# Rotary swap of queries and keys done by 32-row transfers inside SBUF, and the hyena projection's column pairs taken in another order with the transposition moved into its stage

## The reference, cut to what matters

```
q, k, v, g, hy_u, gate_ret, gate_hy = split(h @ w_in + b_in, ...)
# retention: 4 heads of 128 for q and for k; each head is rotated in two halves of 64
def rope_1d(x, ang):                       # x: 64 wide, ang: 32 wide
    x1, x2 = x[..., :32], x[..., 32:]
    return concat([x1 * cos - x2 * sin, x1 * sin + x2 * cos])
q_h = rope_grid(q);  k_h = rope_grid(k) * 128 ** -0.5
...
# hyena: u = hy_u is 1536 wide, three parts of 512
x0, x1, v = split(short_conv(u, conv_w, conv_b), 3)     # 3 taps along the tokens, plus a bias
z = x1 * v
y = long_conv(z) + z * skip
out = x0 * y
```

## Time and profile before

| | us |
|---|---|
| median of 3 runs (lowest, highest) | 4257.39 (4257.15, 4257.42) |
| the profiled execution's own time | 4258.63 |
| its span, first to last instruction | 4256.8 |
| PE busy in the span | 3793.8 (89%) |
| DVE busy | 1520.0 (36%) |
| ACT busy | 1015.0 (24%) |
| mean granted clock of PE (1 is full) | 0.959 |

### The profile page before, as it was taken

One profiled execution on the slowest core, in us unless ns is written; L12 is line 12 of the kernel. 1 busy time (PEld: TensorE's weight loads), 2 busy tenths in 40 slices (PEclk: granted clock), 3 DMA queues, 4 the chain that ended last, 5 costly groups with the idle time before them and its releaser, 6 DMA issues. The chain is left out here.

```text
span 4256.8 us, 96995 instructions
## 1 busy us (share of the span) xinstructions
PE 3793.8 (89%) x42177; PEld 2439.0 (57%) x42177; DVE 1520.0 (36%) x2645; ACT 1015.0 (24%) x2384; POOL 604.8 (14%) x748
## 2 busy tenths in 40 slices
PE   7998899989999889999978998978888799996995
PEld 2443447874444478888854444447777644445774
DVE  5456225552112410000042666545555512222003
ACT  3200100040011122222243442034454211112333
POOL 1120000001100000000010001235555211000112
PEclk9999999999999889999989999989999999997998
DMA  8352311203112389999961001100000111206998
GB/s 293 131 163 79 121 59 60 79 12 70 42 34 93 121 310 393 394 390 395 398 219 25 9 3 45 40 6 5 4 4 4 64 48 52 98 37 226 384 388 317
DMA packets 242335, 597.53 MB, mean 140 GB/s; under 512 B 37097, under 2 KB 149640, under 8 KB 222123
## 3 DMA queue, kind: packets, MB, share of 16 engines
q1 hardware_dynamic: 200867, 471.27, 30.4%
q0 software_dynamic: 19120, 73.68, 5.0%
q10 hardware_dynamic: 22104, 49.00, 3.4%
HBM read 522.85 MB, written 71.05 MB: 140 GB/s over the span
## 5 line engine op out<-in xcount | busy, mean ns | idle before, releaser
L1790 PE MATMUL experts_bank<-experts_uT,ex_wu 128*64 128x96 f32 x9216 | 389.9, 247 | 25.9 <-PE experts_bank L1776 22.2
L1790 PEld LDWEIGHTS experts_bank<-experts_uT,ex_wu 128*64 128x64 f32 x9216 | 383.6, 137 | 42.7 <-issue 42.7
L1863 DVE TENSOR_TENSOR experts_hT<-experts_si,experts_bank 128x384 f32<-128x384 f32 (+1 forms) x68 | 31.3, 460 | 723.6 <-PE experts_bank L1790 723.6
L1790 PE MATMUL experts_bank<-experts_uT,b2z_hT 128*64 128x96 f32 x4096 | 179.1, 249 | 27.3 <-DMA b2z_hT<-in_w 14.8
L1790 PEld LDWEIGHTS experts_bank<-experts_uT,b2z_hT 128*64 128x64 f32 x4096 | 173.4, 139 | 42.2 <-issue 42.2
L1776 PE MATMUL experts_bank<-mixed_T,experts_hT 128*32 128x256 f32 (+1 forms) x2592 | 193.9, 451 | 0.0
L1776 PEld LDWEIGHTS experts_bank<-mixed_T,experts_hT 128*32 128x32 f32 x2592 | 110.4, 110 | 69.6
L1818 ACT ACTIVATE experts_uT<-experts_bank,all_modrun 128x96 f32<-128x96 f32 x296 | 99.3, 439 | 211.6 <-PE experts_bank L1771 211.6
L2413 POOL TENSOR_TENSOR b2z_hT<-b2z_hT,rwkv_level 128x256 f32<-128x256 f32 x192 | 140.2, 763 | 44.3 <-DVE b2z_hT L2892 33.5
L1399 DVE TENSOR_TENSOR merge_u<-merge_bank,merge_sg 128x512 f32<-128x512 f32 x16 | 11.1, 692 | 340.1 <-PE merge_bank L1332 340.1
L3294 PE MATMUL mh_sc<-mla_KTs,mh_QT 128*128 128x512 f32 x256 | 120.7, 594 | 5.9 <-ACT mla_KTs L3339 5.9
(11 more groups left out here) (618 smaller groups left out, 7264.0 us busy)
## 6 DMA issues: line engine op xcount, KB each, us to landing
ex_wu<-in_expert_w SPq DMA_DIRECT2D x72, 2048.0 KB
mixed_T<-in_expert_w SPq DMA_DIRECT2D x36, 2048.0 KB
b2z_hT<-in_w SPq DMA_DIRECT2D x64, 1024.0 KB
b2z_Z<-in_w SPq DMA_DIRECT2D x32, 1024.0 KB
keep_rows<-mix_hyT ACTq DMA_DIRECT2D x27, 768.0 KB, 8.7
keep_rows<-experts_yo ACTq DMA_DIRECT2D x68, 288.0 KB
mix_hT<-in_ada_w POOLq DMA_DIRECT2D x8, 2048.0 KB, 11.8
vg_w<-in_w_in SPq DMA_DIRECT2D x32, 512.0 KB, 4.5
```

Of the source, the lines that this page charges most:

```text
L1790: last = pe.matmul(bk[2 + j][c:c + 64, h * BT:(h + 1) * BT], wu[:, s, j, k, h * P + c:h * P + c + 64], uT[:, s, k, :], start=(k == 0), sto ...
```

## The change

**Queries and keys.** The matrix `rot`, its load and the 8 rotation products of each step are gone. The sign now sits in the sine table (`k_rope1`). When ACT has moved both halves of tile n to `qk`, it waits until DVE is done with tile n-1 and starts four transfers of 32 rows by 1024 columns (128 KB each) from `qk` to `t[:, 1, :]`, each pair of 32-row groups crossed. DVE makes the cosine product meanwhile, waits for the four transfers (`swapped`), makes the sine product over the whole tile in place, and adds. The loops are written out instead of counted, and the phase uses four banks instead of eight; a tile's weights are asked for when the tile two before it is done.

**Hyena.** The six column pairs are taken in the order 2, 4, 3, 5, 0, 1, so x1 and v come first and x0 last. As soon as a tile of v is made, DVE multiplies the tile of x1 by it. Behind the last pair's products and folds PE transposes the gated tiles in the same block, into the same eight banks. For the last pair ACT makes the first tap of both tiles, the tile that is folded first going first, and DVE the other two; then ACT copies the eight banks to `zn`. `phase_hyena_turn` is gone.

```diff
 def phase_qk(...)
         @b.sync
...
+            for n in range(2, TILES):
+                sp.wait_ge(done, 2 * (n - 1))
+                sp.dma_start(wt[:, n % 2, :, :], w[:, :, n * P:(n + 1) * P]).then_inc(wfull[n % 2], 16)
...
         @b.tensor
         def _(pe):
-            pe.sem_inc(wfree, 2)
-            pe.wait_ge(come, 32)
-            with pe.Fori(0, STEPS) as i:
...
-                for s in range(2):
-                    pe.wait_ge(roped, i * 2 + (s + 1))
-                    pe.wait_ge(evac, i * 4 + (2 * s + 6))
-                    for h in range(2):
-                        last = pe.matmul(bk[4 + 2 * s + h][:, :], rot, one(qk[:, bass.ds(i * 2 + s, 1), h * HALF:(h + 1) * HALF]), start=True, stop=True)
-                    last.then_inc(swapped, 1)
+            for n in range(TILES):
+                pe.wait_ge(wfull[n % 2], 16 * (n // 2) + 16)
+                if n >= 2:
+                    pe.wait_ge(evac, 2 * (n - 1))
+                for h in range(2):
+                    for k in range(KT):
+                        last = pe.matmul(bk[2 * (n % 2) + h][:, :], wt[:, n % 2, k, :], xT[:, k, hs[h]], start=(k == 0), stop=(k == KT - 1))
+                    last.then_inc(done, 1)
 
         @b.scalar
...
+            for n in range(TILES):
+                for h in range(2):
+                    act.wait_ge(done, 2 * n + h + 1)
+                    act.activation(qk[:, n, hs[h]], bk[2 * (n % 2) + h][:, :], ACT.Identity, bias=K.cols[:, bcol + n:bcol + n + 1]).then_inc(evac, 1)
+                act.wait_ge(evac, 2 * n + 2)
+                if n:
+                    act.wait_ge(roped, n)
+                for q in range(4):
+                    here, there = 32 * q, 32 * (q ^ 1)
+                    act.dma_start(t[here:here + 32, 1, :], qk[there:there + 32, n, :]).then_inc(swapped, 16)
 
         @b.vector
...
+            for n in range(TILES):
+                scale = sc[:, n // RH:n // RH + 1]
+                dve.wait_ge(evac, 2 * n + 2)
+                if n:
+                    dve.wait_ge(roped, n)
+                dve.scalar_tensor_tensor(t[:, 0, :], qk[:, n, :], scale, cs[:, 0, :], ALU.mult, ALU.mult).then_inc(turned, 1)
+                dve.wait_ge(swapped, 64 * (n + 1))
+                dve.scalar_tensor_tensor(t[:, 1, :], t[:, 1, :], scale, cs[:, 1, :], ALU.mult, ALU.mult).then_inc(turned, 1)
+                dve.wait_ge(turned, 2 * n + 2)
+                dve.tensor_tensor(qk[:, n, :], t[:, 0, :], t[:, 1, :], ALU.add).then_inc(roped, 1)
 
 def phase_taps(...)
+    ORDER = (2, 4, 3, 5, 0, 1)
...
         def _(pe):
             for p in range(npairs):
                 pairs.products(pe, p)
+            pe.wait_ge(gated, 4)
+            pe.wait_ge(pairs.copied, npairs)
+            pe.wait_ge(pairs.folded, 7 * npairs)
+            for par in range(2):
+                for mt in range(4):
+                    for c in range(4):
+                        src = zc[:, 4 + c, :].rearrange("p (n two) -> p two n", two=2)[:, par, mt * P:(mt + 1) * P]
+                        last = pe.transpose(bk[par * 4 + mt][:, c * P:(c + 1) * P], src, K.ident[:, :])
+                    last.then_inc(tr, 1)
 
         @b.scalar
...
+            for n in (1, 0):
+                t = 2 * ORDER[end] + n
+                act.wait_ge(pairs.folded, 7 * end + (6 if n else 7))
+                act.activation(zc[:, t, :], up[:, n, 0:SEQ], ACT.Identity, scale=tap(0, t), bias=tap(3, t)).then_inc(tapped, 1)
+            for n in range(8):
+                act.wait_ge(tr, n + 1)
+                act.activation(zn[:, n, :], bk[n][:, :], ACT.Copy).then_inc(moved, 1)
             act.wait_ge(asided, 16 * len(aside))
 
         @b.vector
...
+                    if p < end:
+                        then(dve.tensor_scalar(o, up[:, n, 0:SEQ], tap(0, t), tap(3, t), ALU.mult, ALU.add))
+                    else:
+                        dve.wait_ge(tapped, x + 1)
...
+                    if t >= 8:
+                        then(last)
+                        dve.tensor_tensor(zc[:, t - 4, :], zc[:, t - 4, :], o, ALU.mult).then_inc(gated, 1)
 
 def constants():
-    c["k_rope1"] = np.stack([np.cos(ang), np.sin(ang)], 1).astype(f)
+    c["k_rope1"] = np.stack([np.cos(ang), sgn * np.sin(ang)], 1).astype(f)
```

More of the change, by code:

```diff
@@ L498, in _ @@
         @b.scalar
         def _(act):
-            act.sem_inc(evac, 4)
-            with act.Fori(0, STEPS) as i:
-                for s in range(2):
-                    for h in range(2):
-                        hold(act, done, i * 4 + (2 * s + h + 1))
-                        act.activation(one(qk[:, bass.ds(i * 2 + s, 1), h * HALF:(h + 1) * HALF]), bk[2 * s + h][:, :], ACT.Identity,
-                                       bias=K.cols[:, bass.ds(i * 2 + (s + bcol), 1)]).then_inc(evac, 1)
+            for n in range(TILES):
[8 more added lines that the diff above has]
+                    act.dma_start(t[here:here + 32, 1, :], qk[there:there + 32, n, :]).then_inc(swapped, 16)
@@ L508, in _ @@
         @b.vector
         def _(dve):
[L510 to L511 removed]
+            dve.wait_ge(come, 16)
             dve.wait_ge(scale_ok, 2)
[L513 to L527 removed]
+            for n in range(TILES):
[8 more added lines that the diff above has]
+                dve.tensor_tensor(qk[:, n, :], t[:, 0, :], t[:, 1, :], ALU.add).then_inc(roped, 1)
@@ L1943, with __init__ @@
     M1, M2, M4, M6, M7, M5, M3 = range(1, 8)
-    def __init__(self, m, hT, slab, bk):
+    def __init__(self, m, hT, slab, bk, order=range(8)):
+        self.order = order
         self.bk, (self.b11, self.b12), (self.b21, self.b22) = bk, *quarters(hT)
@@ L2047, in phase_taps @@
         bk = m.banks(8)
-        pairs = Pairs(m, xT, slab, bk)
-        zero, chain, asided = m.sems("zero", "chain", "asided")
+        pairs = Pairs(m, xT, slab, bk, ORDER)
+        zero, chain, asided, gated, tr, tapped, moved = m.sems("zero", "chain", "asided", "gated", "tr", "tapped", "moved")
         b = m.block()
         each = -(-len(aside) // npairs)
+        end = npairs - 1
         @b.sync
@@ L3655, in constants @@
     sgn = np.concatenate([-np.ones(32), np.ones(32)] * 2)[:, None]
-    c["k_rope1"] = np.stack([np.cos(ang), np.sin(ang)], 1).astype(f)
-    rot = np.zeros((128, 128))
-    for d in range(128):
-        src = d + 32 if d % 64 < 32 else d - 32
-        rot[src, d] = sgn[d, 0]
-    c["k_rot1"] = rot.astype(f)
+    c["k_rope1"] = np.stack([np.cos(ang), sgn * np.sin(ang)], 1).astype(f)
     return c
```

89 lines of the change are left out of this document (19 added, 70 removed).

## The result

| | us |
|---|---|
| median of 4 runs (lowest, highest) | 4213.61 (4209.61, 4219.78) |
| before, beside it: median of 4 runs (lowest, highest) | 4257.27 (4253.63, 4257.42) |
| ratio (95% interval) | 0.9903 (0.9889, 0.9916) |
| span of the profiled execution | 4218.0 |

The kernel is faster by about 1%, 41.3 us (35.8 to 47.3) by the ratio.

A forecast was written before the change was run, and what follows sets the result against it. Serial work between barriers was taken as the bound, PE setting the pace in queries and keys: 18.2 + 13.3 - 1.1 = 30.4 us off 4258.63, less 1.24 for the median, gives 4227.0; range 4223 to 4231, with slow covered swaps 4222 to 4237.

The forecast's parts named there:

- what their ends move by, the total moves by: Changed phases lie one behind the other between barriers, so the total shifts as their ends do; forecast 30.4 us less.
- the 2 us that the range allowed for the phases behind: Allowance either way in the range, because half-speed stretches in the phases behind may fall otherwise.
- 18.2 forecast: Queries and keys: without rotation products and loop waits, the next phase starts at 638.1 instead of 656.27, minus 18.2 us.
- The rule of the Trainium skill: Queries-and-keys swaps: rows 0 to 31 reach half the ports, two transfers nearly serialize; about 4.8 us, total 0.7 longer.
- the row: Profile row for 512 KB stored from SBUF, 2.6 us, taken as the landing of the last tile's four transfers.
- The cover: Queries and keys: a tile's swap and sum take 6.7 of PE's 13.75 us, so seven of eight tiles cost nothing.
- the clock term: Convolution's start: PE idles nearly 8 us instead of 6.15, so a longer half-clock stretch; plus 1.1 us.
- 13.3 was forecast: Hyena projection's end: ACT's last copy ends at 325.5 instead of 338.78, minus 13.3 us.
- Slow, covered swaps: Queries and keys: landing 8.7, issues 1.33, only the last tile pays; 4235.6 us in total; chance 0.12.
- the bounds: Upper bounds for queries-and-keys swaps: landing 8.7 us, issues 1.33 us each; the saving there falls to 9.6 us.
- Swaps as the bound: Queries and keys: swap loop outlasts PE's tile; 4284 us at X = 20; chance 0.04 slower, 0.04 no difference.
- Hyena saves nothing: Hyena projection's end: copies to `zn` or half-speed transposes eat the gain; at worst 3.5 us; no chance given.

The follow-up runs named there:

- e4: Changed kernel with eight fills of a spent tile on GpSimd at the end of queries and keys; ratio 0.9925, median 4225.1 us.
- e5: The kernel before, unaltered, profiled a second time; 3595.7 us from values and gates to the span's end.
- e16: The changed kernel unaltered, third profile; ratio 0.9911, median 4212.97 us.
- e1: The kernel before with only the hyena part of the change; ratio 0.9962.
- e2: The kernel before with only the queries-and-keys (swap) part of the change; ratio 0.9932.
- e8: The kernel before with its queries-and-keys loop written out on four engines, rotation products kept; ratio 0.9991.
- e15: The kernel before with the queries-and-keys loop written out and PE's rotation products left out, table still loaded; ratio 1.0033.
- e9: The changed kernel without the 32-row transfers, so the rotation is left out; ratio 0.9979.
- e12: The changed kernel with the last tile swapped by halves and the convolution's first table requested early; ratio 0.9893, 4211.0 us.
- e3: The changed kernel unaltered, second profile; ratio 0.9912, median 4219.6 us.
- e6: The changed kernel with each of a tile's four transfers cut into four, 16 requests per tile; ratio 0.9937.

## Why the prediction was wrong, and where it was right

**What failed** is the first step, "what their ends move by, the total moves by", and the 2 us that the range allowed for the phases behind. The ends moved by what was forecast, within 2.2 us, and e4 shows that what lies behind starts as much later as the phase ends later; but it also became shorter, by some 8.6 us (the means 3597.0 and 3588.4). 30.4 + 2.2 + 8.6 = 41.2, and 41.3 was measured. That this closes so well is luck, because the two repeats gave 37.5 and 37.9. 5 of the 8.6 lie in the chunks: 569.0 on average with the old products, 563.9 in thirteen profiles with the new code, and PE's issue time there fell by about 6. The rest is spread; no other phase behind differs by more than 1.2 us in the mean. The waits of PE in the chunks, for e5 and for e16 (waited for: total, times, longest):

```profile
PE rc_banks L2433 <- issue: 47.0, 72, 1.6
PE rc_banks L2433 <- DVE rc_xy L2901: 11.8, 12, 2.7
```

```profile
PE rc_banks L2421 <- issue: 38.4, 61, 1.3
PE rc_banks L2421 <- DVE rc_xy L2889: 11.6, 10, 2.9
```

The longest waits for DVE are the same; what shrinks is PE's wait for its own instructions. Why it shrinks is open. It goes with the products in the old loop (e1, e2, e8, e15), but the same edits shift the 256-record places, and that rival is untested. It isn't the loop's form alone, the transfers or the table. Nor is it the chip: three chips ran both codes (e1 to e4, e5 to e8, e9 to e12), with 47.0 to 50.7 us for the old one and 39.4 to 48.7 for the new, e3 being the one above 44. And even without this, untouched phases drift by 5 to 10 us from profile to profile of one kernel (3584.1 to 3593.8 for the changed one), so 2 us was too little for a range.

**Queries and keys: right, to the tenth by some luck.** 18.2 forecast, 18.3 measured. 110.1 us of projections were forecast as 8 x 13.75 + 0.2 = 110.2; the tail from the first request to the sine product was 1.47 + 0.1 + 2.6 = 4.17, measured 4.19. The parts differ and make up for each other: ACT needs 0.51 to 0.94 us per request, so the fourth starts 1.84 us behind the first and not 1.47, but it lands 2.33 us after its start and not 2.6. The rule of the Trainium skill that stood against this ("SBUF — State Buffer", "Door 1: The DMA port swizzle") gave an estimate of 4.8 us from the first issue; the trace says 4.19, nearer to the row than to the rule. But the estimate adds 2 us of fixed time to a rate that the Trainium skill gives there as measured at 1 MiB, so it can count that time twice, and one chain of 4.19 doesn't decide between row and rule. The cover holds as said, with one tile in which DVE waited 8.3 us for the transfers and PE lost nothing.

**Hyena: right in mechanism, 2.2 us too small.** Without the clock term 13.3 was forecast, and 14.4 came: ACT's copies take 0.50 each, not 0.597, and the transposes run at full clock (4.08 us for 3.5). The clock charge of 1.1 us was wrong: I expected PE to pause nearly 8 us ahead of the convolution; it paused 6.11, because the block ended earlier and the request with it, and the stretch at 0.50 was 3.5 us again. Not foreseen was the middle, 2.0 us longer in this profile. It drifts: three profiles of this same kernel gave 177.9, 177.9 and 175.6. Kernels with the old hyena code have 175.5 to 176.5, but for e15 (179.4), and those with the new one are near 178 in seven of twelve profiles, near 175.7 in five; whether the change has a part in that is not shown.

**The rivals.** Slow, covered swaps: no; the last tile's price was 4.2 us, not 12.7. At the bounds that this rival was priced with, it would not have been covered at all: the next rival works out a loop of 15.3 us from the same bounds, and PE needs 13.75 per tile. Swaps as the bound: no, but e6 shows that rival, and its formula holds within 1.6 us. Hyena saves nothing: no.

## What to carry to other kernels

Rotating by transfers costs only the last tile as long as requests, landing and the two DVE steps of one tile fit under PE's next tile; work out that loop and, to shorten what is left, cut the last tile, not all of them. A table that is waited for behind a barrier is worth an early request into a buffer that the stage before has finished with, above all where the pause costs a half-clock stretch as well. When a range is set for a kernel of many phases, the drift of untouched phases between profiles of one kernel belongs in it: take a second profile before believing a small difference. Idle time of PE that a profile puts down to issue can be a wait for instructions: look whether it comes back every so many instructions and ends behind a transfer of an instruction queue. And before reading an edit that is meant to shift code, see in the trace that something shifted.

## What was not expected of the hardware

In a stretch of 565 us with some 34,000 PE instructions, PE waited 38 to 51 us for the instructions themselves: at 59 to 74 of 133 places, 256 instructions apart, for up to 1.6 us each. Products removed at 0.5 ms went with about 6 us less of this at 2.8 ms, and whether they or the shifted places did it is open. Of 32-row transfers within SBUF on one queue, 128 KB land 3.8 us after their request in the median (2.3 in the last tile), 32 KB 1.9 us, while ACT takes 0.6 us to request either, so sixteen small ones cost 10.1 us of ACT's queue and four large ones 2.45.
